# A decoder layer with expert retrieval: query stage and gather stage in one program, the last job shared between two engines, the epilogue in column blocks

## The reference

```python
q = (h2 @ w_q).reshape(b, s, 8, 2, 128)
s1, s2 = q[..., 0, :] @ keys1, q[..., 1, :] @ keys2   # 128 scores each
v1, i1 = top_k(s1, 16); v2, i2 = top_k(s2, 16)
best, pos = top_k(v1 + v2 over all 256 pairs, 16)     # expert = i1 * 128 + i2
gates = softmax(best)
y[t] = sum over 8 heads, 16 experts: gate * gelu(u_tab[e] . h2[t]) * v_tab[e]
out = rmsnorm(x + g2 * y) * final_norm_g
```

## Time and profile before

| what | us |
|---|---|
| median of 3 runs | 1969.32 |
| lowest and highest run | 1966.35, 1971.31 |
| the profiled execution's own time | 1967.97 |
| its span in the trace | 1966.1 |
| TensorE matmul busy | 1467.7 |
| VectorE busy | 1180.6 |
| GpSimd busy | 565.7 |
| ScalarE busy | 408.4 |

### The profile page before, as it was taken

How to read it: one execution, slowest core, us unless ns; L and a number is a source line. 1 busy time by engine, 2 the same in 40 slices (tenths; PEclk the granted TensorE clock), 3 DMA queues, 4 the chain that set the end, 5 groups by cost and what they waited for, 6 DMA issues and landing times.

```text
span 1966.1 us, 14489 instructions
## 1 busy us (share of the span) xinstructions
PE 1467.7 (75%) x5234; PEld 842.4 (43%) x5234; DVE 1180.6 (60%) x1571; ACT 408.4 (21%) x762; POOL 565.7 (29%) x625
## 2 busy tenths in 40 slices
PE   0399998899798067777777777777777777777787
PEld 0289986778798023222322222323222223222233
DVE  6978584687674965555555555556555555554421
ACT  1154342663443011010110110101101011010001
POOL 1000010000010486334333333334334333333320
PEclk9689999999899589999999999999999999999998
DMA  9989795556591999999999999999999999999992
GB/s 377 415 315 403 280 362 222 205 204 248 189 365 44 369 404 422 422 421 422 422 422 421 421 422 421 422 421 422 422 422 422 423 421 421 422 422 421 422 399 107
DMA packets 125043, 717.76 MB, mean 365 GB/s; under 512 B 10502, under 2 KB 14764, under 8 KB 45996
## 3 DMA queue, kind: packets, MB, share of 16 engines
q0 software_dynamic: 82976, 604.02, 74.4%
q1 hardware_dynamic: 41996, 112.81, 15.1%
HBM read 714.69 MB, written 2.10 MB: 365 GB/s over the span
## 4 chain that ended last, share of the span: by engine, by line
DMA 54%; DVE 6%; PE 3%; POOL 3%; issue 1%; ACT 0%; DVEq 0%; ACTq 0%; POOLq 0%
DMA u_rows<-in_peer_u,expert 52%; DVE u_rows L1601 5%; PE ps L1478 3%; DMA v_rows<-in_peer_v,expert 2%; POOL u_rows L1457 1%; POOL v_rows L1457 1%; DVEq L1533 0%; ACT scaled L1497 0%; DVE tk_i L1541 0%; DVE scaled L1614 0%; DVE tk_v L1544 0%; DVE x L1631 0%; DVE tk_v L1539 0%; DVE rest L1542 0%; DVE oh L1566 0%
## 5 line engine op out<-in xcount | busy, mean ns | idle before, releaser
L1478 PE MATMUL ps<-v_rows,diag 128*128 128x512 f32 x2048 | 957.3, 614 | 363.0 <-DMA v_rows<-in_peer_v,expert 261.2
L1601 DVE SCALAR_TENSOR_TENSOR u_rows<-u_rows,h 128x2048 f32<-128x2048 f32 x256 | 586.9, 2292 | 532.7 <-DMA u_rows<-in_peer_u,expert 531.2
L1478 PEld LDWEIGHTS ps<-v_rows,diag 128*128 128x128 f32 x2048 | 377.8, 193 | 941.9 <-issue 471.1
L1457 POOL DMA_INDIRECT u_rows<-in_peer_u,expert x256 | 261.7, 1022 | 678.7 <-DVE u_rows L1601 614.9
L1457 POOL DMA_INDIRECT v_rows<-in_peer_v,expert x256 | 265.1, 1036 | 128.0 <-issue 77.0
L1519 ACT ACTIVATE diag<-ident,hidden 128x128 f32<-128x128 f32 x256 | 90.6, 395 | 576.0 <-PE ps L1478 526.6
L274 POOL DMA_DIRECT2D ada_late<-in_w_ada x64 | 33.8, 529 | 551.4 <-DVE ada_acc L288 293.3
L288 DVE SCALAR_TENSOR_TENSOR ada_acc<-ada_late,cact,ada_acc 128x2048 f32<-128x2048 f32 x60 | 140.7, 2346 | 6.0 <-DMA ada_late<-in_w_ada 5.4
L1490 ACT ACTIVATE hidden<-hidden 128x16 f32<-128x16 f32 x16 | 3.4, 216 | 558.0 <-DVE u_rows L1601 558.0
L557 DVE TENSOR_TENSOR ring_low<-ring,win_high 128x1024 fp32r<-128x1024 f32 (+1 forms) x64 | 74.2, 1170 | 33.7 <-ACT win_high L553 33.5
L553 ACT CAST win_high<-ring 128x1024 fp32r<-128x1024 f32 (+1 forms) x64 | 64.5, 1010 | 88.0 <-PE ps L608 48.0
(11 more groups left out here) (258 smaller groups left out, 1385.9 us busy)
## 6 DMA issues: line engine op xcount, KB each, us to landing
ada_late<-in_w_ada POOLq DMA_DIRECT2D x64, 1024.0 KB, 8.2
ada_early<-in_w_ada SPq DMA_DIRECT2D x32, 1024.0 KB, 17.7
ring<-in_w_in SPq DMA_DIRECT2D x14, 2048.0 KB, 17.2
ring<-in_w_o SPq DMA_DIRECT2D x8, 2048.0 KB, 17.5
ring<-in_w_peer_q SPq DMA_DIRECT2D x8, 2048.0 KB, 10.5
u_rows<-in_peer_u,expert POOLq DMA_INDIRECT x256, 32.2
v_rows<-in_peer_v,expert POOLq DMA_INDIRECT x256, 33.4
ring<-in_w_uq SPq DMA_DIRECT2D x1, 3072.0 KB, 18.9
```

The lines of the kernel that those rows point to most:

```text
L1457: nc.gpsimd.indirect_dma_start(buf[:, :], None, table, bass.IndirectOffsetOnAxis(ap=expert[:, q, k:k + 1], axis=0)).then_inc(done, 16)
L1478: ins = nc.tensor.matmul(ps[:, c, :], diag[n % len(diag)][:, :], buf[:, 512 * c:512 * c + 512], start=(n % half == 0), stop=(n % half == h ...
L1601: nc.vector.scalar_tensor_tensor(out=buf[:, :], in0=buf[:, :], scalar=1.0, in1=h2[:, q // H, :], op0=ALU.mult, op1=ALU.mult, accum_out=hid ...
```

## The change

The query stage and the gather stage become one program. Retrieval of jobs 0 and 1 is put between the pairs 15 to 31, and the dot products of slots 0 to 8 after the pairs 23 to 31. The buffers of the gathers are laid out anew, so that the first four u buffers lie where `w_ada` loads and accumulator were, three in ring slot 0 and the v buffers mostly in ring slot 1. More steps on `w_ada` are done in the earlier programs, token rows move to block 0, scores one or two pairs earlier, the last columns from pair 29 to pair 17. Six slots of the last job are multiplied and summed by VectorE. The last epilogue and the store of the result run in column blocks, and the square root's table is loaded ahead.

```diff
-    u_rows = [at(f"u_rows{b}", A + 8 * KB * b, [P, D]) for b in range(7)]
-    v_rows = [at(f"v_rows{b}", o, [P, D]) for b, o in enumerate([A + (64 + 8 * k) * KB for k in range(4)] + [B + 8 * k * KB for k in range(4)])]
-    scaled = at("scaled", A + 56 * KB, [P, D])
+    u_rows = [at(f"u_rows{b}", A + o * KB, [P, D]) for b, o in enumerate((64, 72, 80, 88, 0, 8, 16))]
+    v_rows = [at(f"v_rows{b}", o, [P, D]) for b, o in enumerate([A + (24 + 8 * k) * KB for k in range(5)] + [B + 8 * k * KB for k in range(3)])]
+    scaled = at("scaled", B + 24 * KB, [P, D])
...
-    gate = small("gate", [P, TT * H, TOPK])
+    gate = small("gate", [P, 4, TOPK])
...
-    ADA_IN, ADA_OUT = 70, 80
+    ADA_IN, ADA_OUT = 74, 86
     ada_after = {}
-    for p in range(6, 37):
-        ada_after[p] = (EARLY + (p - 6) * KC // 31, EARLY + (p - 5) * KC // 31)
-    for p in range(44, 64):
-        ada_after[p] = (48 + (p - 44) * 12 // 20, 48 + (p - 43) * 12 // 20)
+    for p in range(6, 31):
+        ada_after[p] = (EARLY + (p - 6) * KC // 25, EARLY + (p - 5) * KC // 25)
+    for p in range(35, 63):
+        ada_after[p] = (48 + (p - 35) * KC // 28, 48 + (p - 34) * KC // 28)
...
-                    if w.c == 38:
+                    if w.c == 32:
                         ada_cols(2)
 
+            ada_cols(3)
             pe.wait_ge(lat_normed, TT)
...
-            ada_cols(3)
...
-            ada_sums(60, 64)
+            ada_sums(64, 68)
...
-            for k in range(ADA_IN + 3, ADA_OUT):
+            for k in range(ADA_IN + 3, ADA_OUT + 3):
                 ada_load(pool, k)
...
-                    if n == 3 and m == 3:
+                    if n == 2 and m == 3:
                         ada_cols(4)
...
-                    if n in (1, 2) and m in (0, 1, 2, 6, 7):
+                    if (n, m) in ((1, 0), (1, 1), (1, 2), (1, 6), (1, 7), (2, 0), (2, 6), (2, 7), (3, 0), (3, 1), (3, 2), (3, 6)):
                         ada_sum(next(ada))
...
+    BY_VECTOR = tuple(SLOTS - TOPK + k for k in (2, 4, 7, 9, 12, 14))
...
+            for m in range(4):
+                t, c = m // 2, m % 2
+                sp.wait_ge(y_done, m + 1)
+                sp.dma_start(out_view[:, t, 1024 * c:1024 * c + 1024], x2[:, t, 1024 * c:1024 * c + 1024]).then_inc(out_stored, 16)
...
         @block.gpsimd
         def _(pool):
-            for k in range(ADA_OUT, 6 * KC):
+            for k in range(ADA_OUT + 3, 6 * KC):
                 ada_load(pool, k)
...
+            def gather_u(n):
+                if n % TOPK == 0:
+                    pool.wait_ge(experts_ready, n // TOPK + 1)
+                if n == 0:
+                    pool.wait_ge(ada_steps, 6 * KC)
+                if n == 3:
+                    pool.wait_ge(ada_columns, 6)
+                if n == 4:
+                    full(pool, "p5")
+                buf, landed, _ = next_slot(n, u_rows, u_landed)
+                if n >= len(u_rows):
+                    pool.wait_ge(dots, n - len(u_rows) + 1)
+                gather(n, buf, landed, peer_u[0])
+
+            def gather_v(n):
+                if n == 0:
+                    full(pool, "p7")
+                buf, landed, _ = next_slot(n, v_rows, v_landed)
+                if n >= len(v_rows):
+                    used_up(pool, n - len(v_rows))
+                gather(n, buf, landed, peer_v[0])
...
-                    if n == 1:
+                    if n == 0:
                         token_rows(m)
-                    if n and m == 4:
-                        score(2 * n - 2)
-                    if n and m == 5:
-                        score(2 * n - 1)
-                    if w.c == 29:
+                    if n and m in (2, 3):
+                        score(2 * n - 4 + m)
+                    if w.c == 17:
                         ada_cols(5)
...
+            nc.scalar.preload_act_table_set("sqrt_and_others")
+            for c in range(4):
+                square(1, c)
             std(1)
...
+            def serve(n, early):
+
                 q, k = divmod(n, TOPK)
                 dot(n)
                 if k == 0 and q:
                     weights(q - 1)
                 if q + 2 < QJOBS:
-                    for part in range(RETRIEVAL * k // TOPK, RETRIEVAL * (k + 1) // TOPK):
+                    k0 = early if q == 0 else 0
+                    for part in range(RETRIEVAL * (k - k0) // (TOPK - k0), RETRIEVAL * (k - k0 + 1) // (TOPK - k0)):
                         retrieve(part, q + 2)
...
+            first_parts = {c: (0, range(3 * (c - 15), min(3 * (c - 15) + 3, RETRIEVAL))) for c in range(15, 21)}
+            first_parts.update({c: (1, range(RETRIEVAL * (c - 21) // 11, RETRIEVAL * (c - 20) // 11)) for c in range(21, 32)})
+            served = 0
+            ada = iter(range(ADA_OUT, 6 * KC))
+            for n in range(4):
+                for m in range(PAIRS):
+                    c = PAIRS * n + m
+                    if c >= BEGUN:
+                        query_low(dve, n, m)
+                    if c in (3, 5, 7, 8, 9, 10, 11, 12, 13, 14):
+                        ada_sum(next(ada))
+                    if c == 20:
+                        ada_finish(5)
+                    job, parts = first_parts.get(c, (0, ()))
+                    for part in parts:
+                        retrieve(part, job)
+                    if c >= 23:
+                        dot(served)
+                        served += 1
+            for n in range(served, SLOTS):
+                serve(n, served)
             weights(QJOBS - 1)
-            dve.wait_ge(added, SLOTS)
-            take_sums(1)
-            residual(1)
+            y, before = None, 0
+            for n in BY_VECTOR:
+                buf, landed, count = next_slot(n, v_rows, v_landed)
+                w = hidden[:, (QJOBS - 1) % 4, n % TOPK:n % TOPK + 1]
+                dve.wait_ge(landed, count)
+                if y is None:
+                    dve.wait_ge(weighted, QJOBS)
+                    step(nc.vector.tensor_scalar(buf[:, :], buf[:, :], w, None, ALU.mult))
+                else:
+                    nc.vector.scalar_tensor_tensor(out=buf[:, :], in0=buf[:, :], scalar=w, in1=y[:, :], op0=ALU.mult,
+                                                   op1=ALU.add).then_inc(v_used[before % len(v_rows)], 1)
+                    used_up(dve, before)
+                y, before = buf, n
+            step(nc.vector.tensor_tensor(y[:, :], y[:, :], g2b[:, :], ALU.mult))
+            step(nc.vector.tensor_tensor(x2[:, 1, :], x2[:, 1, :], y[:, :], ALU.add))
+            for c in range(4):
+                take_sums(1, c)
+                residual(1, c)
             variance(1)
             normed(1)
```

More of the change, by code:

```diff
@@ L1294, in _, with next_slot, used_up @@
                 query_low(dve, 0, m)
+    QJOBS = TT * H
+    HALF_SLOTS = SLOTS // TT
+    BY_VECTOR = tuple(SLOTS - TOPK + k for k in (2, 4, 7, 9, 12, 14))
+    u_landed = [nc_sem(f"u_rows{b}_landed") for b in range(len(u_rows))]
+    v_landed = [nc_sem(f"v_rows{b}_landed") for b in range(len(v_rows))]
+    v_used = [nc_sem(f"v_rows{b}_used") for b in range(len(v_rows))]
+    experts_ready, shifted, exponents, dots, activated, weighted, diagonal, summed = map(
+        nc_sem, ("experts_ready", "shifted", "exponents", "dots", "activated", "weighted", "diagonal", "summed"))
+    y_taken, y_added, y_squared, y_var, y_std, y_rstd, y_done, out_stored, fg_loaded = map(
+        nc_sem, ("y_taken", "y_added", "y_squared", "y_var", "y_std", "y_rstd", "y_done", "out_stored", "fg_loaded"))
+    def next_slot(n, rows, landed):
+        b, use = n % len(rows), n // len(rows)
+        return rows[b], landed[b], 16 * (use + 1)
+    def used_up(eng, n):
+        eng.wait_ge(v_used[n % len(v_rows)], n // len(v_rows) + 1)
+    by_tensor = [n for n in range(SLOTS) if n not in BY_VECTOR]
     with nc.Block() as block:
@@ L1516, in _ @@
                     n = TOPK * q + k
-                    if n >= len(diag):
-                        act.wait_ge(added, n - len(diag) + 1)
-                    nc.scalar.activation(diag[n % len(diag)][:, :], ident[:, :], ACT.Copy,
-                                         scale=hidden[:, q, k:k + 1]).then_inc(diagonal, 1)
-            squares(1)
+                    if n not in BY_VECTOR:
+                        i = by_tensor.index(n)
+                        if i >= len(diag):
+                            used_up(act, by_tensor[i - len(diag)])
+                        nc.scalar.activation(diag[i % len(diag)][:, :], ident[:, :], ACT.Copy,
+                                             scale=hidden[:, q % 4, k:k + 1]).then_inc(diagonal, 1)
+            nc.scalar.preload_act_table_set("sqrt_and_others")
+            for c in range(4):
+                square(1, c)
             std(1)
@@ L1586, in retrieve @@
                 t, h = divmod(q, H)
+                if part == 0 and t == 0:
+                    copied(dve, f"sc{h}")
                 if part < 8:
@@ L1630, in normed @@
                 dve.wait_ge(y_rstd, t + 1)
```

(11 more changed lines are left out.)

186 lines of the change are left out of this document (82 added, 104 removed).

## The result

The changed kernel takes 1905.76 us (median of four runs, 1900.70 to 1908.28). The kernel before took 1967.92 us on the same chip, so the ratio is 0.968, with a 95% interval of 0.965 to 0.970. The forecast was 1910, in a range of 1897 to 1930. The profiled execution took 1904.93 us, with a span of 1903.0. Of one later kernel, `before_ada`, an execution of 3869.11 us beside eleven of 1965.84 to 1975.12 us is a slow one and is left out.

What follows compares the result with a forecast made beforehand. It took the gather stage to be bound by transfers, so its start, continuity and tail count. Span 1966.1 - 48.6 (start) - 16 (end) + 3 + 1.5 (earlier stages) = 1906; with 1.9 and 1.35 added, 1910 us, range 1897 to 1930.

Steps and rivals of the forecast that it cites:

- What bounds the kernel: Gather stage: bound by transfers, 421 to 423 GB/s without a break from the fifteenth slice to the last but one.
- Start of the stream: Query to gather stage: gathers stream as if full since 598.7 us instead of 647.3, a gain of 48.6 us.
- the second batch: Query stage: gathers from u 4 on wait for the end of pair 23, forecast at 600.4 us.
- VectorE's pace: Query stage from pair 23: VectorE needs 4.4 us a pair for subtraction, retrieval parts and a dot.
- TensorE under it: Query stage from pair 23: TensorE waits for VectorE at 4.4 us a pair, ending about 8 us later.
- The lock: VectorE holding up GpSimd's gather issues: 0 us beyond the old dip, bounds 0 and 10.
- The first rival: Stream starts less full: port lock takes 9 us, early loads 6 more than forecast; 1925 us, chance 0.2.
- Earlier stages: Moved w_ada steps: 3 us lost in the input projection, 1.5 in the query stage, 0 in the output projection.
- The end: From slot 239's landing to the end: 57.3 us instead of 73.3, VectorE deciding; gain 16 us, bounds 9 and 21.
- The sum: Whole kernel: 1966.1 - 48.6 - 16 + 3 + 1.5 = 1906 us of span, 1910 us as the median.
- the rival by which nothing is lost in the earlier stages: No loss in the earlier stages and the last rows ahead; 1900 us, chance 0.1.
- the other rivals: Late tail buffers, 1918 us (0.1); early gathers filling no hole, 1952 (0.03); TensorE's clock falling in gather stage, slower (0.01).

Runs made afterwards that it cites:

- before_ada: The kernel before with only the new order of the w_ada steps; 1969.28 us, ratio 1.000 (0.999 to 1.001) to the kernel before.
- late_dots: The changed kernel with the nine early dot products moved from under the query stage to after it; 1921.01 us.
- psum_dot: The changed kernel with the dots of slots 11 to 127 reading their h2 row from PSUM instead of SBUF; 1902.36 us, one profiled execution.
- after_again: The changed kernel run once more, unaltered, as the control of the later runs; 1907.50 us.

## Why the prediction was right

**What bounds the kernel: right, with a slip.** The slices of the earlier trace rows stand at 421 to 423 GB/s from the sixteenth to the thirty-eighth; the fifteenth has 404 and the last but one 399. No term used the slip.

**Start of the stream: right.** I had 48.6 us, less 1.5 for the query stage, 47.1 together. From the routing start to slot 239 the change needs 46.4 us less (1386.9 against 1340.5), and `late_dots` shows that 13.0 of them are the early dots'. Most steps under it held too: the second batch at 600.19 (600.4), dot 8 ends at 630.5 (632), v 0 at 637.09 (637). Job 0 was ready 4.8 us early, at 580.2 and not 585, which moved only the first four gathers. The 600.19 owes something to luck: pair 18 began at 578.27 and not 581.3, and then the lower clock cost more than I had taken, 12.9 us from there to pair 21 instead of 10.4. VectorE's pace is 35.08 us for the eight dots from 593.13 to 628.21, 4.39 us each; I had 4.4.

**TensorE under it: half right.** I let it wait at 4.4 us a pair from pair 23 on. It waits 4.5 us in all and makes the eight pairs from 596.91 to 626.73 in 3.73 us each, for the copies made ahead last until pair 28. Its last pair starts 4.7 us later than before, not 8. No term of the sum hung on that.

**The lock: right, now for a shown reason.** I took 0 with a bound of 10. `psum_dot` shows about 1 us for the time from 640 us on, and says nothing of the time before. The first rival's mechanism is real, an issue grows from 0.94 to 2.97 us, but its price is not, because GpSimd has the time: from 640 to 705 us 35 instructions keep it busy 54.63 us, 1.56 each, so that two gathers with 0.3 us ahead of each take 3.7 us, under the 4.97 us of their transfers.

**Earlier stages: the step that was off.** I took 3 us lost in the input projection, for its transfers, and 1.5 in the query stage, for the eight steps, 4.5 together. The runs of `before_ada` give 0, at most 2.6. By 210 us TensorE had waited 0.9 us there and not the 2.5 to 3 of my sum (0 to 3.1 in the other profiles with this order). What I had left out is that the moved columns also move the fall of the clock behind them. Its length, which differs between profiles of the same code, makes as much of a difference in the input projection and in the query stage as the terms that I had reckoned. Why the medians come out level is open.

**The end: right.** 57.3 us were forecast, 57.8 and 57.1 measured, with VectorE deciding in the full change and TensorE with five slots. Slot 254 landed 1883.30 - 1845.22 = 38.1 us after slot 239 (37.3 forecast, 37.4 in `after_again`), and VectorE began it at once; its two passes ended at 1890.40, +45.2 (44.5), and TensorE's last sum at 1889.50, +44.3 (43.3). The gain is 15.8 us; 16 was the forecast.

**The sum.** 46.4 + 15.8 + 1.8 for the earlier routing start (mean of 504.6 and 503.6 against 505.9) are the 64.0 us between the spans (1966.1, and the mean of 1903.0 and 1901.1). I had 60.1. The difference is the term of the earlier stages, but the 1.8 itself is scatter: over all nine profiles with this code ahead of it the routing stage starts at 507.0 on average, 1.1 us later than in the one of before. In the medians the gain is 62.2 and 62.6 us, and the forecast from its own median 59.3. That 1905.76 lies between my 1910 and the rival by which nothing is lost in the earlier stages (1900 us) fits: one half of that rival came about, the other half (last rows ahead) did not, and none of the other rivals did. Why the routing start moves by up to 10 us between profiles of nearly one program I have not settled. One part is the fall of the clock in the output projection: the stage takes 97.6 to 99.3 us in the eight profiles with undivided columns that have it and 94.4 to 94.7 in the three that do not.

## What to carry to other kernels

Where a stream of transfers is the limit, three things counted here: when it starts, whether a buffer is ever late, and what is left when it ends. They can be costed apart; here front and tail added up, while the two parts of the tail are worth 2.0 us more together than one by one. Put work of the next stage under the last one even if it slows that one down, where it opens the stream (here 13.0 us were gained by dots that made TensorE wait 4.5), and let every gather wait for the readers of its own buffer, not for the end of a block: here that one wait was worth 5.6 us after the other two edits. Compare profiles between marks that an edit can move, for the stages ahead of them may scatter by more than the edit is worth.

## What the runs showed of the hardware

- An indirect gather is issued in 0.94 us, and in up to 2.97 us when VectorE runs an instruction with two SBUF operands beside it; it then ends some 0.8 us after that instruction. With one of the dot's operands in PSUM it takes 0.94 us again (34 of 35 issues from 640 to 705 us of `psum_dot`, and 1.15 the other). VectorE's instruction is not slowed (2287 and 2292 ns).
- Behind thirty-two matmul records of one column (3.6 us and more) TensorE's granted clock fell to half in 30 of 33 cases, in the middle of stages where it is busy nearly all the time; behind two groups of sixteen with a pair between them it did so in none of nine. I had expected the fall, but not that it could be avoided so cheaply.
- A sum of 16 diagonals moved from TensorE to VectorE in part (six slots) shortened the tail by 11 us, and five slots do as well as six.
